# Two diffusion and sequence blocks on one Trainium2 core: the recurrence's instruction order from a new table of durations and a shorter pace

## The reference, cut to what matters

```
def step(S, inp):
    r_t, w_t, k_t, v_t, kk_t, b_t = inp
    sa = jnp.einsum('bhvk,bhk->bhv', S, kk_t)
    S = (S * w_t[:, :, None, :] - sa[..., None] * b_t[:, :, None, :]
         + v_t[..., None] * k_t[:, :, None, :])
    return S, jnp.einsum('bhvk,bhk->bhv', S, r_t)
```

## Time and profile before

| | us |
|---|---|
| median of 3 runs (lowest, highest) | 3450.59 (3449.07, 3455.3) |
| the profiled execution's own time | 3450.55 |
| its span in the trace | 3448.5 |
| the recurrence in it, about 740 to 1358 us | 618 |

### The profile page before, as it was taken

The page is one execution under the profiler, slowest core; times in us unless marked ns, Lnnn a source line. Parts: engine busy times, 40 slices in busy tenths (PEclk is TensorE's granted clock), DMA queues, the critical chain, the costliest instruction groups (busy, mean ns, idle before and its releaser), DMA issues.

```text
span 3448.5 us, 57984 instructions
## 1 busy us (share of the span) xinstructions
PE 3278.7 (95%) x25525; PEld 2065.6 (60%) x25525; DVE 2078.4 (60%) x3695; ACT 944.9 (27%) x1943; POOL 51.9 (2%) x117
## 2 busy tenths in 40 slices
PE   7998899989999998989999999999999999999998
PEld 3446765558888887444444444446566347777853
DVE  3127855547676775655556567669988665434534
ACT  3246741115455554210000100011111403233310
POOL 2000010000000000000000000000000000000000
PEclk9999999989999999999999999999999999999999
DMA  6010003200000002132111116552111112000021
GB/s 248 0 39 18 1 25 122 103 31 19 4 19 3 3 3 79 71 101 73 67 37 49 37 50 245 202 192 88 32 37 61 32 67 62 25 25 25 1 92 67
DMA packets 116863, 211.81 MB, mean 61 GB/s; under 512 B 6083, under 2 KB 67138, under 8 KB 115970
## 3 DMA queue, kind: packets, MB, share of 16 engines
q1 hardware_dynamic: 106818, 175.08, 15.0%
q10 hardware_dynamic: 9792, 33.02, 2.7%
HBM read 181.86 MB, written 26.21 MB: 60 GB/s over the span
## 4 chain that ended last, share of the span: by engine, by line
PE 81%; DVE 11%; ACT 5%; issue 2%; DMA 1%; ACTq 0%; SPq 0%; DVEq 0%
PE psum_all L66 80%; ACT sbuf_all L72 4%; DVE sbuf_all L81 4%; DVE sbuf_all L91 3%; DVE sbuf_all L99 2%; PE psum_all L111 1%; ACT L72 1%; DMA sbuf_all<-in_x 1%; DVE sbuf_all L105 1%; DVE sbuf_all L88 0%; DVE sbuf_all L102 0%; DMA sbuf_all<-in_w_up 0%; DVE sbuf_all L111 0%; DVE sbuf_all L75 0%; ACTq L61 0%
## 5 line engine op out<-in xcount | busy, mean ns | idle before, releaser
L66 PE MATMUL psum_all<-sbuf_all 64*64 64x64 f32 (+10 forms) x24770 | 3196.3, 316 | 140.9 <-ACT sbuf_all L72 73.6
L66 PEld LDWEIGHTS psum_all<-sbuf_all 64*64 64x64 f32 (+4 forms) x24770 | 1982.6, 155 | 1330.0 <-issue 873.1
L72 ACT ACTIVATE sbuf_all<-psum_all 128x256 f32<-128x256 f32 (+5 forms) x925 | 375.1, 426 | 1519.3 <-PE psum_all L66 1302.5
L81 DVE TENSOR_TENSOR sbuf_all<-sbuf_all 128x512 f32<-128x512 f32 (+9 forms) x911 | 607.5, 709 | 233.2 <-ACT sbuf_all L72 125.9
L91 DVE SCALAR_TENSOR_TENSOR sbuf_all<-sbuf_all 128x520 f32<-128x520 f32 (+8 forms) x783 | 581.4, 776 | 16.9
L72 ACT ACTIVATE sbuf_all<-sbuf_all 128x64 f32<-128x64 f32 (+16 forms) x539 | 306.6, 581 | 575.1 <-DVE sbuf_all L87 208.3
L81 DVE TENSOR_TENSOR sbuf_all<-sbuf_all,psum_all 128x512 f32<-128x512 f32 (+3 forms) x188 | 121.1, 646 | 257.4 <-PE psum_all L66 253.4
L72 ACT ACTIVATE sbuf_all<-psum_all,sbuf_all 128x1280 f32<-128x1280 f32 (+5 forms) x212 | 164.8, 784 | 365.0 <-PE psum_all L66 265.6
L105 DVE COPY_PREDICATED sbuf_all<-sbuf_all,psum_all 128x256 f32<-128x256 int32 (+2 forms) x296 | 143.9, 489 | 63.5 <-PE psum_all L66 59.1
L75 DVE COPY sbuf_all<-psum_all 128x512 f32<-128x512 f32 (+8 forms) x93 | 48.8, 532 | 195.8 <-PE psum_all L66 172.4
L87 DVE TENSOR_SCALAR sbuf_all<-sbuf_all 128x256 f32<-128x256 f32 (+9 forms) x151 | 57.6, 418 | 148.3 <-ACT sbuf_all L72 145.1
(11 more groups left out here) (21 smaller groups left out, 177.3 us busy)
## 6 DMA issues: line engine op xcount, KB each, us to landing
sbuf_all<-in_w_down SPq DMA_DIRECT2D x44, 1024.0 KB, 5.0
sbuf_all<-in_w_mod SPq DMA_DIRECT2D x12, 2048.0 KB, 8.0
sbuf_all<-in_w_up SPq DMA_DIRECT2D x22, 1024.0 KB, 7.7
sbuf_all<-in_w_in SPq DMA_DIRECT2D x6, 2048.0 KB, 9.4
sbuf_all<-in_conv_w_in SPq DMA_DIRECT2D x16, 512.0 KB, 5.6
sbuf_all<-in_gla_w_in SPq DMA_DIRECT2D x8, 1024.0 KB, 5.4
hid_spill<-sbuf_all ACTq DMA_DIRECT2D x9, 512.0 KB, 2.6
sbuf_all<-in_x ACTq DMA_DIRECT2D x2, 2048.0 KB, 20.5
```

Of the source, the lines that this page charges most:

```text
L66: return self.e.matmul(out, lhsT, rhs, start=start, stop=stop, skip_group_check=True)
L72: return self.e.activation(out, in_, func, bias=bias, scale=scale, **kw)
L81: return self.e.tensor_tensor(out, a, b, op) if self.e is not None else Unissued()
```

## The change

It leaves every instruction, every buffer and every dependence as they are. It alters only the numbers from which scan_orders works out the three lists, and how it counts them:

- PACE goes from 4200 to 3500 ns a chunk.
- All durations in scan_steps are replaced. A duration is now the time for which a step holds its engine. What lies between that and the step's signal is a TAIL apart: 165 ns on TensorE, 35 on VectorE, 30 on ScalarE.
- A hop between engines is HOP = 40 ns for all, behind the tail. In the backward pass the hop counts only between different engines, the tail always.
- LATER is an empty table; its loop adds nothing.

The core of the diff (in scan_steps some of some 50 lines that change a number each):

```diff
-PACE = 4200
+PACE = 3500
+TAIL = {"t": 165, "v": 35, "s": 30}
+HOP = 40
+LATER = {}
...
-        step("t", 2500, ("key_norms", j), ("key_squares", j))
+        step("t", 2350, ("key_norms", j), ("key_squares", j))
...
-        for n, ns in enumerate((860, 860, 430)):
+        for n, ns in enumerate((1060, 1060, 500)):
             step("t", ns, ("gates", s, n), *free)
             for lo in (0, LORA):
-                step("s", 610 if n < 2 else 390, ("gate_out", s, lo, n), ("gates", s, n), *free)
+                step("s", 570 if n < 2 else 360, ("gate_out", s, lo, n), ("gates", s, n), *free)
         for part in range(5):
-            step("v", 690, ("sums", s, part), *(("gate_out", s, 0, n) for n in range(3)), *halves("beta", s - 1),
+            step("v", 585, ("sums", s, part), *(("gate_out", s, 0, n) for n in range(3)), *halves("beta", s - 1),
                  *halves("key", s - 1))
-        step("v", 300, ("middle", s), *(("sums", s, part) for part in range(5)), *gone(s - 2))
+        step("v", 270, ("middle", s), *(("sums", s, part) for part in range(5)), *gone(s - 2))
...
-            step("v", 800, ("centre", s, h), ("middle", s))
-            step("v", 800, ("past", s, h), ("centre", s, h))
+            step("v", 780, ("centre", s, h), ("middle", s))
+            step("v", 780, ("past", s, h), ("centre", s, h))
             step("s", 700, ("exp_inverse", s, h), ("past", s, h), ("exp_centred", s, h))
...
-            step("v", 800, ("beta", s, h), ("rates", s, h), ("exp_inverse", s, h), *gone(s - 2))
+            step("v", 780, ("beta", s, h), ("rates", s, h), ("exp_inverse", s, h), *gone(s - 2))
...
-        step("t", 1800, ("bonus", s), *halves("bonus_terms", s))
+        step("t", 1820, ("bonus", s), *halves("bonus_terms", s))
...
-            step("t", 870, ("products", gi, pair), *factors, *([("pass", gi - LANES, 3)] if gi >= LANES else []))
-            step("v", 700, ("mask", gi, pair), ("products", gi, pair))
+            step("t", 885, ("products", gi, pair), *factors, *([("pass", gi - LANES, 3)] if gi >= LANES else []))
+            step("v", 655, ("mask", gi, pair), ("products", gi, pair))
...
-        step("v", 420, ("first", gi), ("mask", gi, 0), ("mask", gi, 1))
-        step("v", 340, ("mirror", gi, 0), ("first", gi))
+        step("v", 410, ("first", gi), ("mask", gi, 0), ("mask", gi, 1))
+        step("v", 410, ("mirror", gi, 0), ("first", gi))
...
-            step("t", 500, ("level_y", gi, li), ("mirror", gi, 0) if li == 1 else ("de_out", gi, li - 1))
-            step("v", 440, ("turn", gi, li), ("level_y", gi, li))
-            step("t", 500, ("level_de", gi, li), ("turn", gi, li), ("mirror", gi, li - 1))
-            step("s", 390, ("de_out", gi, li), ("level_de", gi, li))
+            step("t", 475, ("level_y", gi, li), ("mirror", gi, 0) if li == 1 else ("de_out", gi, li - 1))
+            step("v", 405, ("turn", gi, li), ("level_y", gi, li))
+            step("t", 475, ("level_de", gi, li), ("turn", gi, li), ("mirror", gi, li - 1))
+            step("s", 360, ("de_out", gi, li), ("level_de", gi, li))
...
-            step("t", 600, ("take", gi, ci), ("solve_out", gi), *before, *out)
-            step("s", 240, ("used", gi, ci), ("take", gi, ci))
-            step("t", 270, ("pass", gi, ci), ("used", gi, ci))
+            step("t", 575, ("take", gi, ci), ("solve_out", gi), *before, *out)
+            step("s", 200, ("used", gi, ci), ("take", gi, ci))
+            step("t", 235, ("pass", gi, ci), ("used", gi, ci))
...
-    steps, hop = scan_steps(), {"t": 300, "v": 100, "s": 100}
+    steps = scan_steps()
...
-        due[name] = min([end, *(due[x] - hop[e] for x in followers[name])]) - ns
+        due[name] = min([end, *(due[x] - TAIL[e] - HOP * (steps[x][0] != e) for x in followers[name])]) - ns
+    for name in due:
+        due[name] += LATER.get(name[0], 0)
...
-                at = max(at, ends[out] + hop["v"])
+                at = max(at, ends[out] + HOP)
...
-                at = max(at, ends[user] + hop["t"])
+                at = max(at, ends[user] + HOP)
...
-        end = ends[name] = free[e] = start + steps[name][1]
+        free[e] = start + steps[name][1]
+        ends[name] = free[e] + TAIL[e]
...
-                at = max(ends[y] + hop[steps[y][0]] * (steps[y][0] != steps[x][0]) for y in steps[x][2])
+                at = max(ends[y] + HOP * (steps[y][0] != steps[x][0]) for y in steps[x][2])
```

More of the change, by code:

```diff
@@ L1219, in scan_steps @@
         s = 2 * j - 1
-        step("v", 1000, ("keys", j), *halves("removed", s), *halves("rates", s))
+        step("v", 900, ("keys", j), *halves("removed", s), *halves("rates", s))
         step("s", 1270, ("key_squares", j), ("keys", j), *halves("key", s), *halves("bonus_terms", s))
-        step("t", 2500, ("key_norms", j), ("key_squares", j))
[L1223 to L1226, removed]
+        step("t", 2350, ("key_norms", j), ("key_squares", j))
+        step("s", 190, ("key_roots", j), ("key_norms", j))
+        step("v", 490, ("key_inverse", j), ("key_roots", j))
+        for n, ns in enumerate((640, 640, 390)):
+            step("t", 1000 if n < 2 else 500, ("key_spread", j, n), ("key_inverse", j))
             step("v", ns, ("key_scale", j, n), ("key_spread", j, n))
@@ L1237, in scan_steps @@
                  *halves("key", s - 1))
-        step("v", 300, ("middle", s), *(("sums", s, part) for part in range(5)), *gone(s - 2))
-        step("v", 450, ("gain", s), ("middle", s))
-        step("s", 200, ("exp_gain", s), ("gain", s))
+        step("v", 270, ("middle", s), *(("sums", s, part) for part in range(5)), *gone(s - 2))
+        step("v", 550, ("gain", s), ("middle", s))
+        step("s", 180, ("exp_gain", s), ("gain", s))
         for h in range(2):
-            step("v", 800, ("centre", s, h), ("middle", s))
-            step("v", 800, ("past", s, h), ("centre", s, h))
-            step("s", 700, ("exp_centred", s, h), ("centre", s, h), *gone(s - 2))
+            step("v", 780, ("centre", s, h), ("middle", s))
+            step("v", 780, ("past", s, h), ("centre", s, h))
+            step("s", 720, ("exp_centred", s, h), ("centre", s, h), *gone(s - 2))
@@ L1245, in scan_steps @@
             step("s", 700, ("exp_inverse", s, h), ("past", s, h), ("exp_centred", s, h))
             step("s", 700, ("exp_past", s, h), ("past", s, h))
-            step("v", 1400, ("directed", s, h), *(("gate_out", s, LORA, n) for n in range(3)), ("keys", j),
+            step("v", 1440, ("directed", s, h), *(("gate_out", s, LORA, n) for n in range(3)), ("keys", j),
                  ("key_norms", j), *halves("key", s - 1), *halves("bonus_terms", s - 1))
-            step("v", 800, ("rates", s, h), ("directed", s, h), *(("key_scale", j, n) for n in range(3)))
@@ L1250, in scan_steps @@
-            step("v", 800, ("received", s, h), ("exp_centred", s, h))
-            step("v", 800, ("beta", s, h), ("rates", s, h), ("exp_inverse", s, h), *gone(s - 2))
-            step("v", 800, ("key", s, h), ("directed", s, h), ("exp_inverse", s, h), *gone(s - 2))
-            step("v", 800, ("removed", s, h), ("exp_past", s, h), *(("key_scale", j, n) for n in range(3)))
+            step("v", 780, ("rates", s, h), ("directed", s, h), *(("key_scale", j, n) for n in range(3)))
+            step("v", 780, ("received", s, h), ("exp_centred", s, h))
@@ L1254, in scan_steps @@
+            step("v", 780, ("beta", s, h), ("rates", s, h), ("exp_inverse", s, h), *gone(s - 2))
+            step("v", 780, ("key", s, h), ("directed", s, h), ("exp_inverse", s, h), *gone(s - 2))
+            step("v", 780, ("removed", s, h), ("exp_past", s, h), *(("key_scale", j, n) for n in range(3)))
             step("v", 700, ("bonus_terms", s, h), *halves("removed", s), *halves("directed", s))
-        step("t", 1800, ("bonus", s), *halves("bonus_terms", s))
-        step("v", 200, ("bonus_out", s), ("bonus", s))
+        step("t", 1820, ("bonus", s), *halves("bonus_terms", s))
@@ L1257, in scan_steps @@
+        step("v", 150, ("bonus_out", s), ("bonus", s))
     for gi in groups:
@@ L1282, in scan_steps @@
             out += [("put_out", gi - 3)] if ci == 0 and gi >= 3 and has_output(gi) and has_output(gi - 3) else []
[L1283 to L1285 removed]
+            step("t", 575, ("take", gi, ci), ("solve_out", gi), *before, *out)
+            step("s", 200, ("used", gi, ci), ("take", gi, ci))
+            step("t", 235, ("pass", gi, ci), ("used", gi, ci))
             if not last:
[L1287 removed]
+                step("v", 235, ("state", gi, ci), ("pass", gi, ci), *([] if first else [("kept", gi, ci)]))
             if not first and not last:
[L1289 removed]
+                step("s", 320, ("kept", gi, ci), ("state", *before_chunk(gi, ci)))
         if has_output(gi):
             d = STREAMS[GROUPS[gi][0]][1]
[L1292 removed]
+            step("v" if d else "s", 360, ("put_out", gi), ("pass", gi, 3))
     return steps
 def scan_orders():
[L1300 removed]
+    steps = scan_steps()
```

8 lines of the change are left out of this document (4 added, 4 removed).

## The result

The changed kernel takes 3471.5 us in the median (3460.61 to 3474.55), the kernel before on the same chip 3450.59 (both are medians of five runs): a ratio of 1.005 with a 95% interval of 1.0031 to 1.0069. It is slower by 0.3 to 0.7%, outside my range and on the other side. The profiled execution has a span of 3471.0 us, 22.5 more than before.

What follows compares the result with a forecast made beforehand. It took TensorE's weight loads to bound the kernel, with 84.6 us missing in the 618 us recurrence. Terms -4.5 and -4 gave -8.5 us against 3450.55, so 3442.1 us; range 3425 to 3461, the forecast's own case 3435 to 3448.

Steps and rivals of the forecast that it cites:

- Where the time lies: Whole kernel: only the 618 us recurrence changes, through its 84.6 us without weight loads; 740 us before and 2090.5 behind stay.
- the seams: Seven places in the recurrence, just before or around a new stream's first products, together missing 54.2 us of weight loads.
- Pace and chains: Preparation before the seams: bonus gains 0.085 groups, 1.3 us, on a level step of its group; between 0 and -9, taken -4.5 us.
- A threshold: Order lists near the seams: bonus of stream 1 stays between the same two due times, most lists alike, no large step.
- Truer times: Forward pass of the recurrence: truer latencies cure a fifth of 20.7 us of TensorE's waits on VectorE and ScalarE, -4 us.
- Slower: Rival, chance 0.20: preparation passes on VectorE delay turns and mirrors before the seams, costing 11 us; 3462 us (3454 to 3473).
- Closed by half: Rival, chance 0.13: preparation starts 10 us or more earlier, half the 54.2 us of the seams goes, -27; 3423.5 us.
- Start and end: First and last stretch of the recurrence: 0 us at both, with 1.5 to 3 us either way at the end.

## Why the prediction was wrong

**Where the time lies: right.** The recurrence changed by 21 of the 22.5 us, the stage behind it kept its time, and the loss is in and beside the seams. That late preparation makes them is now shown, by the same three steps moved +10, 0, -15 and -30 us (3503.9, 3471.5, 3436.0, 3419.8 us).

**"Pace and chains": a step that failed.** I worked out from due times that bonus gains 0.085 groups, 1.3 us, against a level step of the same group, and took -4.5 us. The due times were right (bonus of stream 1 is due at 115.44, where I had 115.40), and for the place of bonus they were nearly right: behind the first seam it stays within three places in TensorE's list. The step that failed is to take this one lead for the whole chain. Bonus moved back by 2.7 us on the mean instead of forward by 1.3, but the pace alone does all of that and costs 6 us, and the short latencies alone bring it 0.7 us nearer and cost 24. What they put off is the gates behind it: 6.2 us before, 6.0 with the pace alone, 9.4 in the change, 13.0 with the short latencies alone. By itself the pace measures +6 us, on top of the new table -11; neither is the gain by earlier bonus that the term stood for.

The forward pass asks first which step can start first, and due times only part what is ready together. They are not weak for that, as 15 us of them moved the kernel by 35. But the latencies act in that first question, and my sum let them do no more there than cure waits. The lists tell the two apart, though neither case was timed: with the short latencies in the forward pass alone, the first gates of stream 2 are TensorE's 219th step instead of its 211th; with them in the due times alone they stay the 211th. "A threshold" was right for bonus and wrong for the lists. Of TensorE's 968 steps 126 keep their place, and between the last gates of a stream and its first products there are 11.0 steps on the mean of the seven seams, where there were 18.1.

**"Truer times": the step that cost, wrong in sign.** I put it at -4 us, as a fifth of waits to be cured, with a few us the other way at most. The table alone measures +32 us. The level chain's 2.63 us became 2.27 and nearer to the chip, where the shortest levels take 2.35 us in the trace of the change, and this is the part that cost. The truer durations did gain (6 us, 10 with the pace), about the -4 that I gave this term; the truer latencies took 37 us on top of them (the table alone, +32 us, against the durations alone, -6), and some 30 with the new pace (3471.5 against 3442.8). I read the long latencies as slack: they made the plan keep work back, which is what fills a seam. The turns left there (4.1, 2.6 and 1.0 on the mean) fit that; no run tests it apart from the latencies.

**The clock: left out.** My sum had no term for it, though the earlier trace rows had 0.90 and 0.83 beside the seams. 12.6 us of the growth of the recurrence is weight loads that take longer, in stretches at a granted clock of 0.50 that add up to 68 us, where they were 27. The Trainium skill (TensorE: Matmul & The Clock Gate, A second HAM failure mode) tells of a kernel in which frequent small idle times between groups of matmuls made the clock swing between half and full; the eight stretches in and near the seams, with pauses of up to 2.45 us, agree. By the Trainium skill (Perfetto Trace Analysis, Identifying the Most-Contended Engine) weight-load busy time is what to judge TensorE's headroom by; here that time itself grew by 12.6 us for an equal count, so it has to be read beside the clock.

**The rivals.** "Slower" was right in direction, wrong in mechanism: I had preparation with too much priority, crowding VectorE. The runs with earlier preparation are faster, so in this range it is too little. "Closed by half" named the right lever, bonus 10 us nearer to its terms and -27. With the shift of 15 us bonus came 5.8 us nearer and the kernel 17 us below before; on the kernel before, 30 us of shift brought it 15.8 us nearer for 41 us, gates and norms moving with it. So its size was right, only this change doesn't pull that lever, and an earlier bonus alone doesn't either (in the change it then starts 3.5 us behind its terms, and the kernel is still 6 us above before). Start and end: the start misses 18.0 us where it missed 18.9, the end 4.3 where it missed 4.2, as put down.

**What stays open.** How the 21 us of the recurrence would divide if clock and order could be moved apart: no run holds one and moves the other. And why the table alone (+32 us) is worse than with the shorter pace (+21).

## What to carry to other kernels

A list scheduler that takes what can start first is steered by its latencies as much as by its due times: making them truer can cost more than truer durations gain (here 37 us against 6), I think because slack that kept work in reserve is gone. Before such a table is refined, find the chain whose lateness opens the gaps, and give that chain a lead of its own (here a shift of 40 us in the due time of three steps, 43 us off the kernel); with it the other numbers were worth 8 us at most. When an order goes from idle-free to pausing, count the clock too.

## What I had not expected of the hardware

Short pauses cost twice. In the changed kernel the recurrence had 68 us at the lower clock against 27, though its seams miss only some 9 us more, and in the run with later preparation the clock over the whole recurrence was 0.89. Executions of one and the same order also differ along with it: of five runs of the changed kernel the one with a mean granted clock of 0.979 had a span of 3458.7 us, the two with 0.973 had 3471.0 and 3472.7, while the four runs of the kernel before with early preparation lay at 0.983 to 0.984 and within 2.3 us of each other.
